# A hybrid encoder layer on one core: routing tables moved to other buffers, the first expert's down weights loaded earlier, the expert rows transposed in pieces of 128 and 384, and the router's centring moved

## The reference

```python
def encoder_layer(x, mem, ...):
    proj = jnp.dot(x, w_in)                    # q, k, v of groups A and B, q of group M
    oa = window_attention(...)                 # 8 heads, |t-s| <= 128, sink logit, ALiBi
    ob = neighborhood_attention(...)           # 4 heads on an 8 x 64 grid, relative bias
    om = memory_attention(...)                 # 4 heads over 256 memory tokens
    mixed = jnp.concatenate([group_rms(oa, ...), group_rms(ob, ...), group_rms(om, ...)], axis=-1)
    x = layer_norm(DEEPNORM_ALPHA * x + jnp.dot(mixed, w_out), ln1_g, ln1_b)
    x = layer_norm(DEEPNORM_ALPHA * x + grouped_moe(x, ...), ln2_g, ln2_b)

def grouped_moe(x, w_router, router_bias, w_gate, w_up, w_down):
    scores = jax.nn.sigmoid(jnp.dot(xf, w_router))      # 16 experts in 4 groups
    # the best group by its two best experts; those two experts serve the token
    for e in range(16):
        h = jax.nn.silu(jnp.dot(xf, w_gate[e])) * jnp.dot(xf, w_up[e])    # width 512
        y = y + combine[:, e:e + 1] * jnp.dot(h, w_down[e])
```

## Time and profile before

| | us |
|---|---|
| median of 3 runs (1051.46 to 1054.3) | 1052.74 |
| the profiled execution, its own time | 1052.59 |
| span of its trace, first to last instruction | 1050.9 |
| PE busy | 911.3 |
| DVE busy | 616.2 |
| ACT busy | 524.7 |

### The profile page before, as it was taken

The page is one execution under the profiler, slowest core; times in us unless marked ns, Lnnn a source line. Parts: engine busy times, 40 slices in busy tenths (PEclk is TensorE's granted clock), DMA queues, the critical chain, the costliest instruction groups (busy, mean ns, idle before and its releaser), DMA issues.

```text
span 1050.9 us, 15841 instructions
## 1 busy us (share of the span) xinstructions
PE 911.3 (87%) x4911; PEld 754.6 (72%) x4912; DVE 616.2 (59%) x1177; ACT 524.7 (50%) x968; POOL 189.7 (18%) x264
## 2 busy tenths in 40 slices
PE   5889999899799999989936899999999999999910
PEld 5667888778677888877835688787887878878700
DVE  4345634656634554546678789896645766446248
ACT  3343655542444555453234788785634846346103
POOL 4300001010000102000011244352222232223104
PEclk9999999899999999989857899999999999999965
DMA  8731224143313424102547999999867796672253
GB/s 269 133 68 30 83 59 121 41 149 108 104 41 121 144 100 137 43 21 79 207 156 269 380 378 378 367 379 361 287 203 246 244 342 207 210 241 44 56 180 160
DMA packets 111165, 187.73 MB, mean 179 GB/s; under 512 B 22801, under 2 KB 51712, under 8 KB 111120
## 3 DMA queue, kind: packets, MB, share of 16 engines
q1 hardware_dynamic: 97296, 139.48, 38.0%
q0 software_dynamic: 13824, 47.68, 16.9%
HBM read 159.33 MB, written 28.17 MB: 178 GB/s over the span
## 4 chain that ended last, share of the span: by engine, by line
PE 54%; DVE 8%; DMA 3%; ACT 3%; issue 3%; SPq 1%; DVEq 0%; ACTq 0%; POOL 0%; POOLq 0%
PE O L1736 12%; PE C L1477 10%; PE C L1478 9%; PE C L1479 9%; PE O L1658 3%; PE T L1669 2%; PE S L1512 2%; PE T L1700 2%; PE T L1633 1%; DMA mixing<-in_w_up 1%; PE T L1541 1%; DVE mixing L1462 1%; DVE split_aux L1420 1%; ACT split_aux L1118 1%; DMA mixing<-in_w_down 1%
## 5 line engine op out<-in xcount | busy, mean ns | idle before, releaser
L1399 DVE TENSOR_TENSOR split_main<-mixing,split_main 128x1024 fp32r<-128x1024 f32 x192 | 222.8, 1222 | 55.7 <-ACT split_main L988 52.7
L988 ACT CAST split_main<-mixing 128x1024 fp32r<-128x1024 f32 x192 | 193.6, 1052 | 29.2 <-PE C L1479 9.6
L1736 PE MATMUL O<-split_main,split_aux 128*128 128x512 f32 x552 | 134.1, 399 | 15.8 <-DVE split_aux L1420 15.8
L1477 PE MATMUL C<-split_main,split_aux 128*128 128x512 f32 x368 | 143.9, 391 | 2.6 <-DVE split_aux L1405 2.6
L1479 PE MATMUL C<-split_main,split_aux 128*128 128x512 f32 x368 | 143.9, 391 | 0.0
L1478 PE MATMUL C<-split_main,split_aux 128*128 128x512 f32 x368 | 143.9, 391 | 0.0
L1477 PE MATMUL C<-split_main 128*128 128x512 f32 (+1 forms) x320 | 130.1, 406 | 10.7 <-DVE split_main L1268 6.3
L1736 PEld LDWEIGHTS O<-split_main,split_aux 128*128 128x128 f32 x552 | 103.1, 190 | 42.6 <-DVE split_aux L1420 21.4
L1478 PE MATMUL C<-split_main 128*128 128x512 f32 (+1 forms) x320 | 121.5, 380 | 0.0
L1479 PE MATMUL C<-split_main 128*128 128x512 f32 (+1 forms) x320 | 121.1, 379 | 0.0
L1477 PEld LDWEIGHTS C<-split_main 128*128 128x128 f32 x320 | 62.8, 196 | 30.0 <-issue 11.2
(11 more groups left out here) (273 smaller groups left out, 1437.2 us busy)
## 6 DMA issues: line engine op xcount, KB each, us to landing
mixing<-in_w_gate SPq DMA_DIRECT2D x64, 512.0 KB, 10.0
mixing<-in_w_up SPq DMA_DIRECT2D x64, 512.0 KB, 8.2
mixing<-in_w_down SPq DMA_DIRECT2D x64, 512.0 KB, 8.7
mixing<-in_w_in SPq DMA_DIRECT2D x20, 512.0 KB, 3.7
mixing<-in_w_out SPq DMA_DIRECT2D x16, 512.0 KB, 3.8
mixing<-in_w_mem_kv SPq DMA_DIRECT2D x8, 512.0 KB, 4.8
mixing<-in_w_in SPq DMA_DIRECT2D x16, 256.0 KB, 3.6
x_dram<-x_nat POOLq DMA_DIRECT2D x8, 512.0 KB, 3.0
```

What stands on the lines that cost most here:

```text
L988: nc.scalar.copy(wu[0][:, w, :], raw[:, w, :]).then_inc(unit_hi, 1)
L1399: nc.vector.tensor_tensor(wu[1][:, w, :], raw[:, w, :], wu[0][:, w, :].bitcast(F32), ALU.subtract).then_inc(unit_lo, 1)
L1477: ins = nc.tensor.matmul(out_ap, st[0], mvg[0], start=first, stop=False)
L1736: ins = nc.tensor.matmul(Ob[half][:, :], st[a_], wu[b_][:, KD + f, half * 512:(half + 1) * 512], start=(f == 0 and a_ + b_ == 0), stop=(f ...
```

## The change

It has four parts.

1. The tables of `routing()` leave `scratch` for buffers that the attention no longer uses by then (`vbw`, `vstg`, `va`, `mv`, `probsT`). SP no longer waits for `wslot_done` ahead of unit 8, and ACT casts all 12 units of the first expert in its `H` events, ahead of `xgT_his(0)`.
2. `H_PARTS` splits the rows `h` into 128 and 384 columns, where there were 256 and 256. PE does two of the next tile's eight transposes, then the one of the first piece, then the other six, then the three of the second piece. Block 0 of the down product waits for the first piece, blocks 1 to 3 for the second.
3. `GW` and `K` move from attention steps 8 and 9 of sequence 0 into its output projection; the load of the norm's gain and offset (POOL) moves with `K`.
4. For sequence 0, `bn_aggr` moves from `Y` to `VAR`; `LN` moves one attention step later (`2t + 4`), and `SC` too.

```diff
-            if s == 0 and p == 8:
-                t_unit("GW", s)
-            if s == 0 and p == 9:
-                t_unit("K", s)
...
-                    if p == 2 * t + 3:
+                    if p == 2 * t + 4:
                         ev.append(("LN", s - 1, t))
...
         prepare(s, 4)
+        if s == 0:
+            t_unit("GW", s)
         wo(s, 0, 3, WO_ORDER[0], True)
         prepare(s, 5)
+        if s == 0:
+            t_unit("K", s)
...
-    for t in range(NT):
+    for t in range(UNITS // 2):
         ev.append(("H", s, t))
...
+H_PARTS = (range(0, 1), range(1, KF))
...
-        scratch = mixing[:, 8192:12288]
...
+        rows16 = vbw_flat[:, 1024:2048]
+        rows8 = vstg[:, :, :].rearrange("p a b -> p (a b)")
+        tile_eq = va[:, :, :].rearrange("p a (b c) -> p (a b) c", c=SLOTS)
...
             for w in range(UNITS):
                 if w == 6:
                     sp.wait_ge(chunk_lo, NSEQ * NCH)
-                if w == KD:
-                    sp.wait_ge(wslot_done, 1)
                 load_unit(0, w)
...
             xgT_his(0)
-            hi_units(0, 0, range(KD, UNITS))
             expert(0, first=True)
...
-                    if half == 1:
+                    if half == 1 and s == NSEQ - 1:
                         link(nc.vector.bn_aggr(mvv[:, t, :], stats[:, t, :, :].rearrange("p a b -> p (a b)")))
...
-                for i in range(2):
-                    nc.vector.tensor_tensor(h_sb[:, i * 256:(i + 1) * 256], sg[:, i * 256:(i + 1) * 256],
-                                            Cb[1][:, i * 256:(i + 1) * 256], ALU.mult).then_inc(h_mid, 1)
+                for part in H_PARTS:
+                    cols = slice(part[0] * P, (part[-1] + 1) * P)
+                    nc.vector.tensor_tensor(h_sb[:, cols], sg[:, cols], Cb[1][:, cols], ALU.mult).then_inc(h_mid, 1)
...
-                    transpose_rows(j + 1)
...
+                    transpose_rows(j + 1, 0, 2)
+                    transpose_h(j, 0)
+                    transpose_rows(j + 1, 2, KD)
+                    transpose_h(j, 1)
...
-                        pe.wait_ge(hT_lo, j * 2 + f // 2 + 1)
+                        pe.wait_ge(hT_lo, j * 2 + (f > 0) + 1)
```

More of the change, by code:

```diff
@@ L546, in hT_part @@
         def hT_part(part, i):
-            return hT[part][:, 2 * i:2 * i + 2, :], Sb[i][:, 0:256].rearrange("p (k c) -> p k c", k=2)
+            n = len(H_PARTS[i])
+            f = H_PARTS[i][0]
+            return hT[part][:, f:f + n, :], Sb[i][:, 0:n * P].rearrange("p (k c) -> p k c", k=n)
         def c_dest(kind, g):
@@ L591, in routing @@
             G = TT * NG
[L592 to L595, removed]
+            sel = cut(rows16, 0, TT, NE)
+            w16 = [cut(rows16, 128 * i, G, EG) for i in range(8)]
+            w32 = [rows8[:, 32 * i:32 * (i + 1)] for i in range(6)]
+            w8 = [rows8[:, 256 + 8 * i:256 + 8 * (i + 1)] for i in range(8)]
             selv = w16[0]
-            lo_p = scratch[:, 2176:2176 + SLOTS]
+            lo_p = rows8[:, 640:640 + SLOTS]
             rev4 = w16[7]
-            thr = cut(scratch, 1408, NE, TT)
-            one16, tnum = scratch[:, 1584:1600], scratch[:, 1648:1656]
+            thr = cut(rows8, 384, NE, TT)
+            one16, tnum = rows8[:, 560:576], rows8[:, 624:632]
             for i in range(EG):
@@ L651, in routing @@
             dve.wait_ge(rank_done, 1)
-            cmp = cut(scratch, 512, NE, TT)
+            cmp = cut(rows16, 512, NE, TT)
             link(nc.vector.tensor_tensor(cmp, Ob[0][:, 128:128 + NE].unsqueeze(2).to_broadcast([P, NE, TT]), thr, ALU.is_gt))
-            ntl, cum, base = (scratch[:, 1536 + 16 * i:1552 + 16 * i] for i in range(3))
+            ntl, cum, base = (rows8[:, 512 + 16 * i:528 + 16 * i] for i in range(3))
             link(nc.vector.tensor_reduce(ntl, cmp, AX.X, ALU.add))
@@ L702, in slot_weight_parts @@
             N2 = 2 * TT
-            tile_eq = cut(scratch, 1664, N2, SLOTS)
-            rest = [scratch[:, 2240 + 16 * i:2256 + 16 * i] for i in range(3)]
-            part = [scratch[:, 2288 + 8 * i:2296 + 8 * i].bitcast(BF16) for i in range(3)]
+            rest = [rows8[:, 704 + 16 * i:720 + 16 * i] for i in range(3)]
+            part = [rows8[:, 752 + 8 * i:760 + 8 * i].bitcast(BF16) for i in range(3)]
             link(nc.vector.tensor_scalar(rest[0], wts[:, :, :].rearrange("p c t -> p (c t)"), 1.0 / ALPHA, None, ALU.mult))
@@ L858, in _ @@
                         .then_inc(vbw_loaded, 16)
-                elif what == "N" and s == 0 and ev[2] == "M":
-                    pool.wait_ge(o_drained[1], 1)
+                elif what == "K":
                     pool.wait_ge(gains_ready, 1)
@@ L1352, in _ @@
                 elif what == "VAR":
+                    if s < NSEQ - 1:
+                        for t in range(NT):
+                            link(nc.vector.bn_aggr(mvv[:, t, :], stats[:, t, :, :].rearrange("p a b -> p (a b)")))
                     link(nc.vector.tensor_scalar(nv[:, 0:NT], mvv[:, 0:NT, 1], EPS, None, ALU.add))
@@ L1695, in _, with transpose_rows, transpose_h @@
             ins.then_inc(wslot_psum, 1)
-            def transpose_rows(j):
-                pe.wait_ge(xg_loaded, j * 16 + 16)
-                for k in range(KD):
+            def transpose_rows(j, k0, k1):
+                if k0 == 0:
+                    pe.wait_ge(xg_loaded, j * 16 + 16)
+                for k in range(k0, k1):
                     ins = nc.tensor.transpose(Tb[k // 4][:, (k % 4) * P:(k % 4 + 1) * P], xg[:, k * P:(k + 1) * P], ident[:, :])
-                ins.then_inc(xgT_psum, 1)
+                if k1 == KD:
+                    ins.then_inc(xgT_psum, 1)
+            def transpose_h(j, i):
+                pe.wait_ge(h_mid, j * 2 + 2 + i + 1)
+                for f in H_PARTS[i]:
+                    ins = nc.tensor.transpose(Sb[i][:, (f - H_PARTS[i][0]) * P:(f - H_PARTS[i][0] + 1) * P],
+                                              h_sb[:, f * P:(f + 1) * P], ident[:, :])
+                ins.then_inc(hT_psum, 1)
             def unit_wait(e, w):
@@ L1720, in _ @@
                         ins.then_inc(units_used, 1)
-                    transpose_rows(j + 1)
-                    for i in range(2):
-                        pe.wait_ge(h_mid, j * 2 + 2 + i + 1)
-                        for f in range(2):
-                            ins = nc.tensor.transpose(Sb[i][:, f * P:(f + 1) * P],
-                                                      h_sb[:, (2 * i + f) * P:(2 * i + f + 1) * P], ident[:, :])
-                        ins.then_inc(hT_psum, 1)
+                    transpose_rows(j + 1, 0, 2)
+                    transpose_h(j, 0)
+                    transpose_rows(j + 1, 2, KD)
+                    transpose_h(j, 1)
                     pe.wait_ge(y_half[0], j + 1)
```

21 lines of the change are left out of this document (10 added, 11 removed).

## The result

The changed kernel takes 1040.39 us (median of 6 runs, 1038.31 to 1045.84), the kernel before 1053.52 (6 runs beside them, 1051.46 to 1055.86): a ratio of 0.989 with a 95% interval of 0.987 to 0.9911, about 1.1% faster. The forecast was 1041. The profiled execution took 1038.31 us, its span is 1036.6. The sum came out right, but two of its terms did not, and they cancel in part. Lines of `kernel.py` are two to eight higher than before: the multiplication of `h` is L1418, its subtractions L1422, the down product L1744. The transposes of `h` stand in a function of their own now, L1710 (L1725 before).

A forecast was written before the change was run, and what follows sets the result against it. PE paces the tiles, with the vector engine nearly as much the bound in one-tile experts. Savings 1.0 + 2.3 + 0.4 + 0.4 + 7.7 = 11.8 us from 1052.59 give 1040.8, said as 1041; range 1038 to 1044.

The forecast's parts named there:

- Two-tile tiles: Tiles behind expert 7, led by PE: down product starts 0.55 us earlier, about 18.1 us per tile, 7.7 us saved.
- One-tile experts: Experts 2 to 7 and 11: vector engine's round grows 0.21 to 18.65 us, the present pitch, so no gain.
- The term of 0.6: Expert 7: 0.6 us taken back of ACT's 0.93 us wait for an up unit, as loads run ahead.
- The first rival: One-tile experts: the vector engine doesn't hold them, seven more tiles gain 0.55 us each, total 1037 us; chance 0.13.
- the reading over the whole span: Vector engine counted unsaturated at 59% busy over the whole kernel, so all 23 tiles gain 0.55 us, ending near 1037.
- the late second piece: Down product: second piece 0.65 us later than worked out, PE-led tiles gain only 0.2 us, total 1046 us; chance 0.15.
- Expert 0: First expert: earlier down-weight loads bring the multiplication of h forward by 2.3 us.
- the loop's entry costs 0.8: First expert: 0.8 us of vector idle between nine subtractions and five more, ahead of the multiplication of h.
- my upper bound of 3.1: First expert: largest gain allowed for the earlier loads, 3.1 us, if the loop's entry costs nothing.
- I keep the price of the half clock as it is: First expert: PE's gap stays long, so its following run at half clock costs the same as before.
- Front: Before the experts: K's wait -0.61, new wait +0.7, wait at 269 us -0.96; about 1 us saved.
- the new wait of 0.7: Front: GW's vector work ahead of Y delays the next weights' low parts, PE waits 0.7 us (0 to 1.4).

The follow-up runs named there:

- c2: Changed kernel with two pieces of 256 columns instead of 128 and 384, new transpose order kept; 1047.55 us, ratio 0.9954.
- a4: Kernel before with part 4 alone (bn_aggr in VAR, LN and SC one step later); 1054.16 us, ratio 1.0017.
- c1: Changed kernel with all eight transposes of the next rows ahead of the first piece of h, sizes kept; 1041.22 us, ratio 0.9888.
- b3: Changed kernel with one vector subtraction (next expert's unit 5) moved between the two subtractions of h; 1039.56 us, ratio 0.9885.
- b4: Changed kernel with one vector subtraction (next expert's unit 5) moved between h's second subtraction and the next rows' split; 1040.3 us, ratio 0.9888.
- a1: Kernel before with part 1 alone (tables moved, first expert's down weights loaded and cast early); 1048.66 us, ratio 0.9953.

## Why the prediction was right, step by step

**Two-tile tiles: right.** 18.10 to 18.13 forecast as 18.1, no wait inside the down product; -7.3 to -7.45 for -7.7. `c2` shows that the small first piece carries most of it.

**One-tile experts: mechanism right, size wrong.** "The round grows by 0.21, from 18.44 to 18.65, and that is the present pitch." It grew to 18.85: the vector engine gets the next rows 3.18 us behind the multiplication (631.60 to 634.78), not 2.96. The mis-sized term is PE's: I counted every transpose at 0.109 us, but the lone one of the first piece takes 0.17 to the next begin (707.38 to 707.55), not 0.11, and the three of the second 0.49 (708.20), not 0.33; that is the 0.22. With the slack already used, experts 3 to 6 and 11 lose 0.2 each; expert 2 loses 0.55, with 1.09 us idle ahead of its low parts instead of 0.78, and why is open. Expert 7 gains 0.24, but not as forecast: ACT still waits there for an up unit in the second profile (1.09 us at 706.44, 0.93 before), and `a4`, without the earlier loads, loses nothing there. The term of 0.6 isn't shown. That is 1.1 us lost from O1 to O7, where I had 1.0 gained. The first rival (all tiles gain, 1037) falls, and with it the reading over the whole span; so does the late second piece, as no down product waits inside. The Trainium skill ("Perfetto Trace Analysis", section "Optimizing Scalar/DVE Operations") advises larger operations for a saturated engine, and breaking up those of one that isn't saturated but holds up others. I had the trace side with its first half. The loss doesn't bear that out: before and after, the vector engine does two pieces of the same 512 columns, and with the new sizes alone (`c1`) a one-tile expert is no slower. What lengthened the round is the order on PE, the mechanism that I had forecast. `b3` and `b4` show that the vector engine was the bound there and also how little is behind it: with it out of the way the loads are the next bound, and take the gain back.

**Expert 0: two mis-sized terms.** The multiplication of `h` came 3.25 us earlier, not 2.3: "the loop's entry costs 0.8" was wrong for the first entry, where the fourteen subtractions run without a gap; my upper bound of 3.1 was the better value. I left out that tile 0 also gains from the pieces (`h` to O0 is 1.40 us). And "I keep the price of the half clock as it is" was wrong: it is gone, and the down product of tile 0 takes 5.80 us instead of 7.52, most of the 1.95 us from O0 to O1.

**Front: the waits were right, the sum can't be seen.** K's wait is gone, the one at 269 us fell by 0.99 (0.96 forecast), the new wait of 0.7 that I charged for GW did not come; 1.5 us in all, for 1.0. The clock hides it: the first matmul of the routing's count begins at 532.80 to 542.64 us over the 13 profiles of these kernels, 538.80 in the second profile of the changed kernel and 539.49 before.

**Sum.** Expert 0 and the stretch behind it gave 3.8 us more than forecast, experts 2 to 7 2.1 less; the rest agrees within 0.5 in the second profile. That the forecast lay 0.6 us off the median is in part this cancelling, and that part is luck.

**Open.** Whether the clock falls in expert 0 is not sorted by the length of PE's gap: it fell behind 2.32 us (`c1`), 2.45 (`a1`) and 3.14 (`c2`) and stayed up behind 2.2 to 3.0 in all six profiles that have the changed kernel's order and sizes with the earlier loads. The order alone doesn't decide it, since `c2` has the changed kernel's order (behind the longest of these gaps); the rest is open.

## What to carry to other kernels

Where the bound changes from stage to stage, price an edit by each stage's own round, and ask for the slack of the engine behind the leading one: here 0.2 us on the vector engine, and behind it loads that ran late within six experts. A right total proves no term: profile a kernel twice before a stretch is put down to the change. Part size from order: the smaller first piece paid or cost nothing in both kinds of tile; bringing it forward ahead of other work paid where PE led, and cost where the vector engine waited for what it put off.

## What the runs showed of the hardware

**Half clock at the same waits, for different lengths.** Behind the wait of 3.10 us ahead of the projections of sequence 1 the same work, up to the end of PE's next wait for `probs`, took 15.25 to 17.93 us over 13 profiles. At the short end (the changed kernel, then 15.27 in its second profile) the granted clock was 1.00; in `c2`, which is the same program up to there, the work took 17.93 and the clock had fallen (0.50, the 1.2 GHz level, from 284 to 288 us):

```profile
284.00:302.00 18.00, 15.59 (x75) 12.01 (x76) 5.62 (x9) 5.38 (x12) 0.00 (x0) 1.00 0.32 84
```

```profile
284.00:302.00 18.00, 16.21 (x62) 12.49 (x62) 4.79 (x8) 3.46 (x5) 0.00 (x0) 0.82 0.21 59
```

Behind that wait for `probs` (1.73 and 1.74 us) the two executions of the changed kernel part: from 285 to 310 us the clock is 1.00 in the first and 0.93 in the second.

```profile
285.00:310.00 25.00, 23.26 (x125) 18.38 (x123) 9.66 (x28) 10.07 (x24) 0.00 (x0) 1.00 0.23 61
```

```profile
285.00:310.00 25.00, 21.41 (x104) 16.71 (x106) 9.65 (x27) 7.49 (x19) 0.00 (x0) 0.93 0.25 64
```

**A small GpSimd operation that ends with a row of vector operations.** In 2 of 13 profiles the first `idxs` operation took 8.11 and 6.95 us. It ended at 589.67 and 593.89; the vector engine's row of twelve subtractions without a gap ended at 589.62 and 593.85. In the other profiles it took 0.19 to 1.31. Of all 299 such operations two more took over 1.31, 2.19 (in the kernel before) and 2.41 (`c2`), and these too end 0.04 and 0.05 us behind a row of subtractions. GpSimd's line, then the vector engine's row, in `c2`:

```profile
586.94 6.95 POOL L919 TENSOR_TENSOR idxs<-idx,izero 128x1 int32<-128x1 int32 x1 [8.20 <-ACT x_nat L1125]
```

```profile
580.13 13.72 DVE L1401 TENSOR_TENSOR split_main<-mixing,split_main 128x1024 fp32r<-128x1024 f32 x12 [0.39 <-ACT split_main L988]
```

The Trainium skill ("SBUF — State Buffer", section "SBUF: two separate sides") says that a vector operation with two SBUF inputs and a GpSimd operation that reads SBUF lock each other out of a shared port for one whole instruction. The other 295 would agree: one subtraction of 1.14 us and the shortest such operation, 0.18, make 1.32. A hold over six or seven subtractions is more than the page states. That the port is the cause here is likely by the ends, but no run shows it, and why it comes only sometimes was not tried.
